# Adding expert results in DRAM instead of in SBUF: a hybrid SSD and mixture-of-experts layer on one core

## The chip, the cores and the metric

The kernel runs on one core of one Trainium2 chip. The metric is device time in microseconds (us) of one execution, here the median of three runs. The core has TensorE (PE; PEld is its weight load), VectorE (DVE), ScalarE (ACT), GpSimd (POOL) and SyncE (SP), and 16 DMA engines that all queues share. In the views a "q" behind an engine's name (SPq, POOLq) is its instruction queue: issuing a transfer or waiting.

## The reference

One inference layer over 528 prompt rows (16 learned meta rows and 512) and 64 sample rows, 592 rows of 1024 in all. The change touches only the mixture of experts at its end:

```python
def _hier_moe(h, ...):
    p_grp = softmax(t @ w_rg + b_rg);  g_sel = argmax(p_grp)          # one of 4 groups
    le = (t @ w_re + b_re)[group g_sel];  top_v, top_i = top_k(softmax(le), 2)
    top_v = top_v / sum(top_v);  gate = top_v * g_prob                # two experts of that one group
    for g in range(N_EGROUPS):
        act = silu(t @ w_gate[g]) * (t @ w_up[g]) * gate[:, g, :, None]
        out = out + einsum('tef,efd->td', act, w_down[g])
x = x + mixer ; x = x + HierMoE(RMSNorm(x)) ; final RMSNorm
```

There are 32 experts (4 groups of 8) of width 256. Every row goes to two experts, both of the same group. All data are fp32.

## The kernel before

**Stages.** Up to about 1000 us the kernel computes the projections, the short convolution and the state-space branch. Then come the output projection (added into `x2`, the residual rows in SBUF, five tiles of 128 rows, the last of 80), the router, 16 pairs of experts, and the end: summing up, the final norm, the stores.

**Router.** DVE finds the two experts of every row (`m1`, `m2`) and its place within each expert. PE multiplies the one-hot places `at_slot` with `tok_of` (L874), which gives for each slot of an expert the row that sits in it. The first 64 slots of an expert are its *main* part (`MAIN`), the next 32 its *over* part (`OVER`). From this come the indices `gid_main`, `gid_over` for gathering rows and `sid_main`, `sid_over` for scattering results. Slots without a row have an index out of bounds and move nothing, apart from one harmless row (`DUMP`). `tok_of` has two halves, since a row's first result goes to row t of `y_tok` and its second to row 640 + t. A last branch, for an expert with over 96 rows, isn't taken with these data.

**Expert pairs** (`for p in range(PAIRS)`, experts 2p and 2p + 1). PE: gate and up matmuls of main (L944), transposes of the next pair's rows (L920), gate and up of over (L957), transposes of h (L965, L973), down of main into the bank `acc[1]` (L983), down of over into `pS` (L991). ACT applies Silu and copies the transposed rows; DVE multiplies, and copies both results from PSUM to `ye_main` (L1392) and `ye_over` (L1394), double buffered. POOL gathers the rows of pair p + 3 (L1890), then scatters the main results (L1907), waits until they have landed, scatters the over results (L1911), and waits for those before it scatters for the next pair. DVE may write `ye_main` of pair p only when both scatters of pair p - 2 have landed (`ye_out`). SP loads the weights two pairs ahead: gate and up (L518) once PE has done the gate and up matmuls of pair p - 2, down (L521) once it has done its down matmuls.

**End.** When both scatters of the last pair have landed, DVE passes the branch and releases SP by `f_skip`. SP loads ten tiles (two for each tile of rows) from `y_tok` (L555). DVE computes x2 = x2 + y * gate twice for each tile (L1429), ACT the root of the mean square (L1454, L1455), DVE the normed row (L1421, L1422), and SP stores it.

**y_tok fill.** ACT fills `y_tok` once with finite numbers in four transfers during the state-space stage (L1572), DRAM to DRAM.

Of the kernel before, what the change touches and what calls it, by code (L numbers as in the profile page):

```python
# [12 lines left out]
P = 128  # L13
# [38 lines left out]
Y_ROWS, DUMP, NO_TOKEN = 640, 1232, 2048  # L52
# [7 lines left out]
def build(nc, ins, outs):  # L60
    ctx = ExitStack()
    with ctx:
# [141 lines left out]
        tokback, b = carve(b, [2, TILES], big, B5)  # L204
# [3 lines left out]
        at_slot, _ = carve(3 * WE, [2 * TILES, CAP])  # L208
        tok_of, _ = carve(24 * T, [2 * TILES, 2, NE], big, B5)
# [23 lines left out]
        y_in = [carve(D * n, [D])[0] for n in range(2 * TILES)]  # L233
# [4 lines left out]
        def expert_slot(u):  # L238
# [7 lines left out]
        y_tok = nc.dram_tensor("y_tok", [DUMP + 1, D], F32).ap()  # L246
        y_half = y_tok.rearrange("r (h c) -> (r h) c", h=2)
# [51 lines left out]
        y_fill, m_end = sem("y_fill"), sem("m_end")  # L299
# [4 lines left out]
        f_w, f_id, f_cast, f_x, f_tr, f_xe, f_gu, f_silu, f_act, f_dn, f_ye, f_out, f_skip = (  # L304
            sem(n) for n in ("f_w", "f_id", "f_cast", "f_x", "f_tr", "f_xe", "f_gu", "f_silu", "f_act", "f_dn", "f_ye",
                             "f_out", "f_skip"))
        g_in = [sem(f"g_in{i}") for i in range(TILES)]
        z_ss, z_sd, z_y, y_out = (sem(n) for n in ("z_ss", "z_sd", "z_y", "y_out"))
# [103 lines left out]
        def _(sp):  # L412
# [103 lines left out]
            def load_gate_up(e):  # L516
                for part, w in zip(wexp[e % 4][0:2], (wg, wu)):
                    sp.dma_start(part, w[e]).then_inc(gu_in[e // 2 % 2], 16)  # L518

            def load_down(e):  # L520
                sp.dma_start(wexp[e % 4][2], wd[e]).then_inc(dn_in[e // 2 % 2], 16)  # L521
# [69 lines left out]
        def _(pe):  # L591
# [275 lines left out]

            pe.wait_ge(r_sel, 1)
            for bank_, size, at, count in ((pS, MAIN, 0, 2), (pT, OVER, MAIN, 4)):
                for n in range(2):  # L870
                    for i in range(TILES):
                        r = ROWS[i]
                        for q in range(count):
                            m = nc.tensor.matmul(bank_[size * q:size * q + size, 0:2 * PAIRS], at_slot[0:r, n * TILES + i, at:at + size],  # L874
                                                 tok_of[0:r, n * TILES + i, :, q % 2:NE:2], start=n + i == 0,
                                                 stop=i == TILES - 1 and n == 1)
# [55 lines left out]
            pe.wait_ge(s_tl, 8)  # L932
            turn_main(0)
            pe.wait_ge(r_ids, 3)
            turn_over(0)
            for p in range(PAIRS):
# [39 lines left out]

                pe.wait_ge(dn_in[p % 2], 32 * (p // 2 + 1))
                if p >= 1:
                    pe.wait_ge(m_ye, 2 * (p - 1) + 1)
                for h in range(2):  # L980
                    for ft in range(FK):
                        for j in range(2):
                            m = nc.tensor.matmul(acc[1][main_of(j), h, :], hT_main[:, ft, main_of(j)],  # L983
                                                 wexp[(2 * p + j) % 4][2][:, ft, h * 512:(h + 1) * 512],
                                                 start=ft == 0, stop=ft == FK - 1)
                m.then_inc(m_dn, 1)
                pe.wait_ge(m_hc, 2 * p + 2)
                for ft in range(FK):
                    for q in range(4):
                        j, h = q % 2, q // 2  # L990
                        m = nc.tensor.matmul(pS[over_of(q), :], hT_over[:, ft, over_of(j)],  # L991
                                             wexp[(2 * p + j) % 4][2][:, ft, h * 512:(h + 1) * 512],
                                             start=ft == 0, stop=ft == FK - 1)
                m.then_inc(m_dn, 1)
# [4 lines left out]
            with pe.If(n_most > CAP):  # L999
                with pe.Fori(0, NE) as e:  # L1000
                    with pe.Fori(0, ROUNDS) as r:
                        n = e * ROUNDS + r
                        pe.wait_ge(f_x, n * 16 + 16)
                        to_rows(0, f_tr)
                        pe.wait_ge(f_w, n * 48 + 48)
                        pe.wait_ge(f_xe, n + 1)
                        gate_up(0, 0, pT, f_gu)
                        pe.wait_ge(f_act, n + 1)
                        down(0, 0, down_banks[0], f_dn)
# [3 lines left out]
        def _(dve):  # L1013
# [313 lines left out]
            for n, m_ in enumerate((m1_, m2_)):  # L1327
                link(v.tensor_tensor(tok_of[:, n * TILES:(n + 1) * TILES, 0, :], m_.rearrange(fl), wide(tokback[:, 0, :], NE), ALU.mult))
                link(v.tensor_tensor(tok_of[:, n * TILES:(n + 1) * TILES, 1, :], m_.rearrange(fl), wide(tokback[:, n, :], NE), ALU.mult))
# [16 lines left out]
            v.tensor_scalar(sid_main[:, :], pS[:, PAIRS:2 * PAIRS], float(NO_TOKEN), empty, ALU.add, ALU.min)  # L1346
            x = v.tensor_scalar(sid_f, pT[:, PAIRS:2 * PAIRS], 2.0, half, ALU.mult, ALU.add)
# [11 lines left out]
            link(v.tensor_tensor(gate[:, 1, :], gate[:, 0, :], ev, ALU.mult))  # L1359

            dve.wait_ge(r_ids, 3)
            for n, m_ in enumerate((m1_, m2_)):
# [12 lines left out]
                link(v.tensor_tensor(t_, gate[:, n, :], gate_later[:, n, :], ALU.subtract))  # L1375
                link(v.tensor_copy(gate[:, n, :], gate_later[:, n, :]))
                link(v.tensor_copy(gate_later[:, n, :], t_))
            v.tensor_copy(most[0:1, 0:1], cmax[0:1, 0:1]).then_inc(r_slot, 1)

            for p in range(PAIRS):  # L1380
# [15 lines left out]
            for s in range(2):  # L1396
                dve.wait_ge(ye_out[s], 32 * PAIRS // 2)
            n_most = dve.value_load(most[0:1, 0:1], min_val=0, max_val=T)
            with dve.If(n_most > CAP):
                with dve.Fori(0, NE) as e:  # L1400
                    with dve.Fori(0, ROUNDS) as r:
                        n = e * ROUNDS + r
                        dve.wait_ge(f_silu, n + 1)
                        v.tensor_tensor(gs[0], gs[0], pT[:, FK * CAP:2 * FK * CAP].rearrange("p (a b) -> p a b", a=FK),
                                        ALU.mult).then_inc(f_act, 1)
                        dve.wait_ge(f_dn, n + 1)
# [18 lines left out]
            for i in range(TILES):  # L1425
                r = ROWS[i]
                dve.wait_ge(g_in[i], 32)
                for n in range(2):
                    x = v.scalar_tensor_tensor(x2[0:r, i, :], y_in[2 * i + n][0:r, :], gate[0:r, n, i:i + 1], x2[0:r, i, :],  # L1429
                                               ALU.mult, ALU.add)  # L1430
                    if n == 0:
                        link(x)
                x.then_inc(z_ss, 1)
                if i >= 1:
                    finish(i - 1)
            finish(TILES - 1)
# [527 lines left out]
```

## Time and profile before

| | |
|---|---|
| median of 3 runs (lowest, highest) | 1428.02 us (1427.01, 1428.05) |
| the profiled execution: its time, its span | 1430.2 us, 1428.5 us |
| PE busy | 1324.7 us, 93% of the span |
| DVE, ACT, POOL busy | 567.5, 377.9, 457.0 us |
| DMA | 209.75 MB, mean 147 GB/s |
| mean granted clock of TensorE | 0.953 of full speed |

The span runs from the first to the last instruction. Full speed of TensorE is 2.4 GHz; a granted clock of 0.5 is its level of 1.2 GHz.

### The profile page before, as it was taken

To read this page: it belongs to the slowest core of one execution; us is meant where nothing else is said; L and a number is where in the kernel's file an instruction comes from. 1 tells how busy PE (TensorE), PEld (TensorE's weight loads), DVE (VectorE), ACT (ScalarE), POOL (GpSimd) and SP (SyncE) were. 2 spreads that over 40 slices of the span, in tenths; PEclk is the share of its full clock that TensorE was granted. 3 is DMA by queue.
4 is the path that set the end of the run, shared out by engine and by line. 5 is a ranking of instruction groups with operands and counts; after the bars stand their busy time and mean duration, and the time that the engine had idled before them with its cause. 6 is when DMAs were issued, how large, how long until landed. Compare 5 with 4: busy or idle time off the path is not lost.

```text
span 1428.5 us, 23149 instructions
## 1 busy us (share of the span) xinstructions
PE 1324.7 (93%) x9087; PEld 1027.3 (72%) x9087; DVE 567.5 (40%) x816; ACT 377.9 (26%) x574; POOL 457.0 (32%) x380
## 2 busy tenths in 40 slices
PE   4999999999989999998999999999987999999990
PEld 4999999999759877975987799994474444444430
DVE  5444441026566754955676550011153111111115
ACT  4212124344234324333342531210121111101102
POOL 5444432345333533533252454330002112122110
PEclk8999999999989999999999999999956999999995
DMA  5223222235107303520631222337612999999925
GB/s 144 75 75 87 74 68 65 78 84 151 48 13 186 109 0 110 132 65 7 182 104 43 81 74 75 89 104 267 279 49 67 363 368 374 370 360 376 378 97 203
DMA packets 179334, 209.75 MB, mean 147 GB/s; under 512 B 12988, under 2 KB 154428, under 8 KB 170896
## 3 DMA queue, kind: packets, MB, share of 16 engines
q1 hardware_dynamic: 167970, 187.97, 40.2%
q10 hardware_dynamic: 4134, 11.11, 2.2%
q0 software_dynamic: 7168, 9.81, 1.9%
q8 instruction: 44, 0.72, 0.2%
q14 instruction: 18, 0.14, 0.0%
HBM read 196.93 MB, written 32.34 MB: 160 GB/s over the span
## 4 chain that ended last, share of the span: by engine, by line
PE 75%; DVE 12%; issue 4%; ACT 3%; DMA 3%; SPq 1%; DVEq 1%; ACTq 0%; POOLq 0%; POOL 0%
PE acc L584 36%; PE pT L944 8%; PE acc L819 5%; PE pS L957 4%; PE acc L983 4%; DVE area L1149 4%; PE pY L747 2%; PE pS L991 2%; PE pS L691 2%; DMA ring<-in_w_in 1%; PE acc L920 1%; PE acc L713 1%; DVE big L1220 1%; PE pY L927 1%; PE pS L753 1%
## 5 line engine op out<-in xcount | busy, mean ns | idle before, releaser
L584 PE MATMUL acc<-h_parts,ring_parts 128*128 128x328 f32 (+1 forms) x3840 | 551.5, 305 | 12.6 <-DVE h_parts L1047 6.9
L584 PEld LDWEIGHTS acc<-h_parts,ring_parts 128*128 128x128 f32 x3840 | 537.7, 192 | 29.0 <-issue 28.2
L1736 POOL TENSOR_TENSOR ring_parts<-ring,ring_parts 128x1024 fp32r<-128x1024 f32 x104 | 263.2, 2531 | 419.3 <-ACT ring_parts L1468 419.3
L1468 ACT ACTIVATE ring_parts<-ring 128x1024 fp32r<-128x1024 f32 x104 | 110.0, 1058 | 371.1 <-PE acc L584 353.6
L944 PE MATMUL pT<-area,big 128*64 128x512 f32 x384 | 116.1, 611 | 0.2 <-ACT big L1665 0.2
L584 PE MATMUL acc<-u_parts,ring_parts 128*128 128x264 f32 (+1 forms) x640 | 109.4, 299 | 0.0
L584 PEld LDWEIGHTS acc<-u_parts,ring_parts 128*128 128x128 f32 x640 | 96.4, 188 | 0.0
L1149 DVE SCALAR_TENSOR_TENSOR area<-area,xvec 128x616 f32<-128x616 f32 x72 | 90.1, 1252 | 10.5 <-DVE area L1147 0.6
L944 PEld LDWEIGHTS pT<-area,big 128*64 128x64 f32 x384 | 35.5, 140 | 78.8 <-issue 78.8
L584 PE MATMUL acc<-area_parts,ring_parts 128*128 128x264 f32 (+1 forms) x512 | 91.1, 299 | 0.0
L584 PEld LDWEIGHTS acc<-area_parts,ring_parts 128*128 128x128 f32 x512 | 78.4, 188 | 0.0
L1890 POOL DMA_INDIRECT big<-h_rows,gid_main x16 | 16.7, 1043 | 161.9 <-DVE big L1351 107.6
L957 PE MATMUL pS<-area,big 128*32 128x256 f32 x768 | 58.5, 381 | 0.0
L983 PE MATMUL acc<-area,big 128*64 128x512 f32 x192 | 58.4, 598 | 0.0
L944 PE MATMUL pT<-ring,big 128*64 128x512 f32 x128 | 56.6, 595 | 0.0
L1677 ACT ACTIVATE big<-pT 128x256 f32<-128x256 f32 x16 | 6.1, 384 | 190.3 <-PE pT L944 190.3
L1817 POOL TENSOR_TENSOR area<-m_le,da 128x512 f32<-128x512 f32 (+1 forms) x40 | 41.1, 1031 | 47.1 <-PE pS L691 47.1
L1911 POOL DMA_INDIRECT y_tok<-big,sid_over x16 | 16.0, 998 | 125.1 <-DMA y_tok<-big,sid_main 125.1
L1240 DVE TENSOR_TENSOR area<-acc,area 128x528 f32<-128x528 f32 x8 | 5.7, 707 | 115.7 <-PE acc L584 115.7
L1382 DVE TENSOR_TENSOR big<-big,pT 128x256 f32<-128x256 f32 x16 | 6.7, 421 | 111.5 <-ACT big L1677 111.5
L691 PE MATMUL pS<-area,m_gt 128*128 128x512 f32 (+1 forms) x80 | 39.1, 570 | 12.8 <-ACT area L1581 12.8
L1180 DVE TENSOR_TENSOR area<-area 128x512 f32<-128x512 f32 (+1 forms) x40 | 35.8, 903 | 32.3 <-ACT area L1581 30.8
(332 smaller groups left out, 1708.5 us busy)
## 6 DMA issues: line engine op xcount, KB each, us to landing
ring<-in_w_in SPq DMA_DIRECT2D x80, 512.0 KB, 4.1
area<-in_w_gate SPq DMA_DIRECT2D x24, 1024.0 KB, 6.3
area<-in_w_up SPq DMA_DIRECT2D x24, 1024.0 KB, 9.3
area<-in_w_down SPq DMA_DIRECT2D x24, 1024.0 KB, 11.5
area<-in_state_ssm SPq DMA_DIRECT2D x16, 512.0 KB, 7.0
out<-area SPq DMA_DIRECT2D x16, 512.0 KB, 5.3
ring<-in_w_ssd_out SPq DMA_DIRECT2D x16, 512.0 KB, 4.2
ring<-in_w_gate SPq DMA_DIRECT2D x8, 1024.0 KB, 11.5
```

The costliest lines, as they stand in the source:

```text
L584: m = nc.tensor.matmul(acc[a][:, h, 0:n], w[s][:, k, :], x[:, k, h * HALF:h * HALF + n], start=first and k == 0 and w is w_hi and x is hi, ...
L691: nc.tensor.matmul(pS[0:r, 0:4 * r], gt[0:r, 0:r], rbuf[0:r, q, 0:4 * r], start=True, stop=True).then_inc(p_seg, 1)
L747: m = nc.tensor.matmul(pY[0:r, h * HD:(h + 1) * HD], wts[0:r, h // 4, (h % 4) * r:(h % 4 + 1) * r], xdt[0:r, i % 2, h * HD:(h + 1) * HD], ...
L819: m = nc.tensor.matmul(acc[n % 4 // 2][0:ROWS[i], n % 2, :], mT[:, k, tok(i)], wo[h][:, k, :], start=k == 0, stop=k == 7)
L944: m = nc.tensor.matmul(pT[main_of(j), :], xT_[:, k, main_of(j)], gate_up_w(2 * p + j, k), start=k == 0, stop=k == 7)
L957: m = nc.tensor.matmul(pS[over_of(q), 0:FE], xT_[:, k, at:at + OVER], wexp[(2 * p + j) % 4][n][:, k, :], start=k == 0, stop=k == 7)
L983: m = nc.tensor.matmul(acc[1][main_of(j), h, :], hT_main[:, ft, main_of(j)], wexp[(2 * p + j) % 4][2][:, ft, h * 512:(h + 1) * 512], start ...
L1149: x = v.scalar_tensor_tensor(o_, raw[:, c % 2, n:n + XCONV], w[:, 0, n:n + 1], o_, ALU.mult, ALU.add)
L1180: v.tensor_tensor(w, w, cbm[0:r, 0:r].unsqueeze(1).broadcast_to([r, 4, r]), ALU.mult).then_inc(s_w, 1)
L1468: a_.activation(w_hi[b % 2], w_raw[b % 2], ACT.Copy).then_inc(hi_done, 1)
L1736: gp.tensor_tensor(w_lo[b % 2], w_raw[b % 2], w_hi[b % 2].bitcast(F32), ALU.subtract).then_inc(lo_done, 1)
L1817: gp.tensor_tensor(rbuf[0:r, q, 0:4 * r].rearrange("p (h c) -> p h c", h=4), le[0:r, 0:r].unsqueeze(1).broadcast_to([r, 4, r]), da[0:r, i, ...
```

## The change

- Results are weighted as they leave PSUM: instead of a copy, DVE multiplies by a gate for each slot (`gate_main`, `gate_over`). Those gates come from a second selection on PE, `at_slot` times `gate_of` (m1 and m2 times the gates), 60 small matmuls into `acc[1]`, which PE runs before it transposes the first pair's rows.
- `y_tok` becomes `y_sum` with 593 rows. SP fills it with the residual rows `x2` (5 stores, and one for the spare row) after the output projection. The ACT fills go.
- Both scatters of a pair add to what stands in DRAM (`compute_op=ALU.add`).
- A pair is made of one expert of one group and one of another (`expert_of`), so that no row occurs twice in one transfer. `tok_of` has one half instead of two.
- In the last pair the over results go first and the main results second.
- At the end SP waits for the last scatters itself and loads five tiles from `y_sum` straight into `x2`. The ten weighted sums on DVE go.
- Semaphores of the branch that isn't taken are merged.

```diff
+            def expert_of(n):
+                return n // 16 * 16 + n % 2 * EPG + n // 2 % EPG
...
+            for i in range(TILES):
+                sp.wait_ge(r_x2, TILES + i + 1)
+                sp.dma_start(y_sum[tok(i), :], x2[0:ROWS[i], i, :]).then_inc(y_fill, 16)
+            sp.dma_start(y_sum[DUMP:DUMP + 1, :], x2[0:1, 0, :]).then_inc(y_fill, 16)
             for p in range(2, PAIRS):
                 sp.wait_ge(m_gu, 2 * (p - 2) + 2)
...
+            for s in range(2):
+                sp.wait_ge(ye_out[s], 32 * PAIRS // 2)
+            for i in range(TILES):
+                sp.dma_start(x2[0:ROWS[i], i, :], y_sum[tok(i), :]).then_inc(g_in[i], 16)
             sp.wait_ge(m_end, 1)
...
-            sp.wait_ge(f_skip, 1)
-            for s in range(2):
-                sp.wait_ge(ye_out[s], 32 * PAIRS // 2)
-            for i in range(TILES):
-                for n in range(2):
-                    at = n * Y_ROWS + i * P
-                    sp.dma_start(y_in[2 * i + n][0:ROWS[i], :], y_tok[at:at + ROWS[i], :]).then_inc(g_in[i], 16)
...
             pe.wait_ge(s_tl, 8)
+            pe.wait_ge(r_gate, 1)
+            for h, size, at, count in ((0, MAIN, 0, 2), (1, OVER, MAIN, 4)):
+                for n in range(2):
+                    for i in range(TILES):
+                        r = ROWS[i]
+                        for q in range(count):
+                            m = nc.tensor.matmul(acc[1][size * q:size * q + size, h, 0:PAIRS],
+                                                 at_slot[0:r, n * TILES + i, at:at + size],
+                                                 of_pairs(gate_of[0:r, n * TILES + i, :], q % 2), start=n + i == 0,
+                                                 stop=i == TILES - 1 and n == 1)
+            m.then_inc(r_gs, 1)
             turn_main(0)
...
                 pe.wait_ge(dn_in[p % 2], 32 * (p // 2 + 1))
+                if p == 0:
+                    pe.wait_ge(r_gs, 2)
                 if p >= 1:
                     pe.wait_ge(m_ye, 2 * (p - 1) + 1)
+                if p < PAIRS - 1:
+                    down_main()
+                    down_over()
+                else:
+                    down_over()
+                    down_main()
...
+            for n, m_ in enumerate((m1_, m2_)):
+                x = v.tensor_tensor(gate_of[:, n * TILES:(n + 1) * TILES, :], m_.rearrange(fl), wide(gate[:, n, :], NE), ALU.mult)
+            x.then_inc(r_gate, 1)
...
-                dve.wait_ge(m_dn, 2 * p + 1)
-                v.tensor_copy(ye_main[p % 2], acc[1].rearrange("p a b -> p (a b)")).then_inc(m_ye, 1)
-                dve.wait_ge(m_dn, 2 * p + 2)
-                v.tensor_copy(ye_over[p % 2], pS[:, :]).then_inc(m_ye, 1)
+                results = [(ye_main[p % 2], acc[1].rearrange("p a b -> p (a b)"), gate_main), (ye_over[p % 2], pS[:, :], gate_over)]
+                for n, (to, of, by) in enumerate(results if p < PAIRS - 1 else results[::-1]):
+                    dve.wait_ge(m_dn, 2 * p + n + 1)
+                    v.tensor_scalar(to, of, by[:, p:p + 1], None, ALU.mult).then_inc(m_ye, 1)
...
-                act.dma_start(y_tok[bass.ds(g * (DUMP // GROUPS), DUMP // GROUPS), :], ins["x_prompt"][0][0:DUMP // GROUPS, :]
-                              ).then_inc(y_fill, 16)
...
-                pool.indirect_dma_start(y_tok[:, :], bass.IndirectOffsetOnAxis(ap=sid_main[:, p:p + 1], axis=0),
-                                        ye_main[p % 2], None, bounds_check=DUMP, oob_is_err=False).then_inc(ye_out[p % 2], 16)
...
+                results = [(y_sum, sid_main, ye_main[p % 2], DUMP), (y_half, sid_over, ye_over[p % 2], 2 * DUMP + 1)]
+                for n, (to, index, of, bound) in enumerate(results if p < PAIRS - 1 else results[::-1]):
+                    pool.wait_ge(m_ye, 2 * p + n + 1)
+                    if n == 1:
+                        pool.wait_ge(ye_out[p % 2], 32 * (p // 2) + 16)
+                    pool.indirect_dma_start(to[:, :], bass.IndirectOffsetOnAxis(ap=index[:, p:p + 1], axis=0), of, None,
+                                            bounds_check=bound, oob_is_err=False, compute_op=ALU.add).then_inc(ye_out[p % 2], 16)
```

## Rows read from the trace of the kernel before

**Rows 1.** Chain of waits, expert stage: start us, us, what.

```profile
1127.94 7.02 PE pT L944 x32
...
1144.90 1.85 PE pS L991 x16
1146.76 7.02 PE pT L944 x32
```

**Rows 2.** By stretch: us; busy PE, PEld, DVE, ACT, POOL; clock, DMA share, GB/s.

```profile
1125.00:1200.00 75.00, 75.00 (x594) 31.92 (x592) 13.90 (x24) 9.53 (x16) 15.76 (x17) 1.00 0.93 363
...
1392.00:1394.00 2.00, 0.00 (x0) 0.00 (x0) 0.00 (x0) 0.00 (x0) 0.00 (x0) 0.86 0.36 139
```

**Rows 3.** Timeline of POOL: start us, us, what, idle before and releaser.

```profile
1109.43 1.02 POOL L1907 DMA_INDIRECT y_tok<-big,sid_main  x1 [2.92 <-DVE big L1392]
1118.64 1.00 POOL L1911 DMA_INDIRECT y_tok<-big,sid_over  x1 [8.20 <-DMA y_tok<-big,sid_main]
```

**Rows 4.** DMA, 1125 to 1300 us: a queue's share; transfers, KB, us to landing.

```profile
q0 software_dynamic: 4176, 5.78, 8.9%
...
ring<-in_w_up SPq DMA_DIRECT2D x4, 1024.0 KB, 14.3
...
y_tok<-big,sid_main POOLq DMA_INDIRECT x10, 8.5
y_tok<-big,sid_over POOLq DMA_INDIRECT x9, 3.9
```

**Rows 5.** Timeline of SP: the first load of pair 2.

```profile
1102.08 0.33 SPq L518 DMA_DIRECT2D area<-in_w_gate  x1
```

**Rows 6.** Chain of waits after the last pair's main down matmuls.

```profile
1388.44 1.24 DVE big L1392
...
1390.52 3.15 DMA y_tok<-big,sid_main
...
1394.52 3.01 DMA y_tok<-big,sid_over
...
1399.21 5.30 DMA area<-y_tok
...
1408.34 1.28 ACT L1455
...
1423.51 1.28 DVE big L1422
```

**Rows 7.** Groups of instructions: busy us, mean ns, idle before.

```profile
L1429 DVE SCALAR_TENSOR_TENSOR big<-area,gate,big 128x1024 f32<-128x1024 f32 (+1 forms) x10 | 12.8, 1282 | 13.8 <-DMA area<-y_tok 13.6
...
L1382 DVE TENSOR_TENSOR big<-big,pT 128x256 f32<-128x256 f32 x16 | 6.7, 421 | 111.5 <-ACT big L1677 111.5
```

**Rows 8.** The ten loads of L555.

```profile
DMA to landing us min/median/max: 3.9/8.0/11.9
```

**Rows 9.** Timeline of DVE: the reciprocal of one tile at the end.

```profile
1421.69 0.15 DVE L1421 RECIPROCAL stat<-stat 128x1 f32<-128x1 f32 x1
```

**Rows 10.** Chain of waits, router and first pair.

```profile
1074.51 2.35 PE pS L874 x40
1076.85 1.23 PE pT L874 x80
...
1084.32 1.96 PE acc L920 x8
...
1087.53 9.81 PE pT L944 x32
```

**Rows 11.** Timeline of DVE in the router: the second gate.

```profile
1080.25 0.16 DVE L1359 TENSOR_TENSOR gate<-gate,big 128x5 f32<-128x5 f32 x1
```

**Rows 12.** By stretch, columns as in rows 2: within the first pair's gate matmuls.

```profile
1093.00:1094.00 1.00, 1.00 (x6) 0.31 (x4) 0.00 (x0) 0.00 (x0) 0.00 (x0) 0.97 0.00 0
```

**Rows 13.** Timeline of ACT beside one fill of y_tok.

```profile
354.34 0.67 ACTq L1572 DMA_DIRECT2D y_tok<-in_x_prompt  x1
...
356.31 0.27 ACT L1577 ACTIVATE area<-pO 128x128 f32<-128x128 f32 x1
```

More of the change, by code:

```diff
@@ L514, in load_expert, with load_gate_up, load_down @@
                     sp.dma_start(part, src).then_inc(done_sem, 16)
[L516 to L521, printed above, removed]
+            def expert_of(n):
+                return n // 16 * 16 + n % 2 * EPG + n // 2 % EPG
+            def load_gate_up(n):
+                for part, w in zip(wexp[n % 4][0:2], (wg, wu)):
+                    sp.dma_start(part, w[expert_of(n)]).then_inc(gu_in[n // 2 % 2], 16)
+            def load_down(n):
+                sp.dma_start(wexp[n % 4][2], wd[expert_of(n)]).then_inc(dn_in[n // 2 % 2], 16)
             for e in (0, 3):
@@ L873, in _ @@
                         for q in range(count):
-                            m = nc.tensor.matmul(bank_[size * q:size * q + size, 0:2 * PAIRS], at_slot[0:r, n * TILES + i, at:at + size],
-                                                 tok_of[0:r, n * TILES + i, :, q % 2:NE:2], start=n + i == 0,
+                            m = nc.tensor.matmul(bank_[size * q:size * q + size, 0:PAIRS], at_slot[0:r, n * TILES + i, at:at + size],
+                                                 of_pairs(tok_of[0:r, n * TILES + i, :], q % 2), start=n + i == 0,
                                                  stop=i == TILES - 1 and n == 1)
@@ L975, in _, with down_main @@
                 m.then_inc(m_ht, 1)
+                def down_main():
+                    for h in range(2):
+                        for ft in range(FK):
+                            for j in range(2):
+                                m = nc.tensor.matmul(acc[1][main_of(j), h, :], hT_main[:, ft, main_of(j)],
+                                                     wexp[(2 * p + j) % 4][2][:, ft, h * 512:(h + 1) * 512],
+                                                     start=ft == 0, stop=ft == FK - 1)
+                    m.then_inc(m_dn, 1)
@@ new lines, in down_over @@
+                def down_over():
+                    pe.wait_ge(m_hc, 2 * p + 2)
+                    for ft in range(FK):
+                        for q in range(4):
+                            j, h = q % 2, q // 2
+                            m = nc.tensor.matmul(pS[over_of(q), :], hT_over[:, ft, over_of(j)],
+                                                 wexp[(2 * p + j) % 4][2][:, ft, h * 512:(h + 1) * 512],
+                                                 start=ft == 0, stop=ft == FK - 1)
+                    m.then_inc(m_dn, 1)
@@ L986, in _ @@
[L986 to L994, printed above, removed]
+                if p < PAIRS - 1:
[4 more added lines that the diff above has]
+                    down_main()
@@ L1345, in _ @@
                             ).then_inc(r_ids, 1)
-            v.tensor_scalar(sid_main[:, :], pS[:, PAIRS:2 * PAIRS], float(NO_TOKEN), empty, ALU.add, ALU.min)
-            x = v.tensor_scalar(sid_f, pT[:, PAIRS:2 * PAIRS], 2.0, half, ALU.mult, ALU.add)
+            v.tensor_scalar(sid_main[:, :], pS[:, 0:PAIRS], float(NO_TOKEN), empty, ALU.add, ALU.min)
+            x = v.tensor_scalar(sid_f, pT[:, 0:PAIRS], 2.0, half, ALU.mult, ALU.add)
             link(x)
@@ L1425, in _ @@
             for i in range(TILES):
[L1426 to L1436, printed above, removed]
+                finish(i)
         @block.scalar
@@ L1697, in _ @@
                         act.wait_ge(f_out, n * 16 + 17)
+            act.wait_ge(f_skip, 1)
             for i in range(TILES):
-                act.wait_ge(z_ss, i + 1)
+                act.wait_ge(g_in[i], 16)
                 root(i, x2[0:ROWS[i], i, :], sqj, z_sd)
```

81 lines of the change are left out of this document (37 added, 44 removed).

## The prediction

> **What bounds the kernel now.** Four views, in this order. The busy time by stretch first: between 1125 and 1200 us PE is busy in all 75 us at a granted clock of 1.00, and the DMA engines at a share of 0.93 [rows 2]. Two resources are nearly full, so the question is which sets the pace. The chain of waits answers: pair after pair it names matmuls alone, and the main gate matmuls of one pair start 18.8 us after those of the last (1127.94, 1146.76) [rows 1]. So PE sets the pace of the expert stage. DMA has 7% to spare there, and anything that adds DMA work or latency has to be priced against that. Third, the timeline of POOL, for the scatters: a serial chain beside PE's. Last, the chain of waits after the last matmuls, where nothing overlaps: from 1388.4 to 1428.5 us each step lies on the path [rows 6], so a microsecond there is a microsecond of the result.
>
> **The end.** Before: the main product leaves PSUM at 1388.44, its scatter starts on POOL at 1390.52 and lands 3.15 later, the over scatter starts at 1394.52 and lands 3.01 later, at 1397.5; the branch, f_skip and the issue take until 1399.21; the first tile's two loads 5.30; then two sums of 1.28 each [rows 6, 7], the square, ACT's table load of 1.28 (at 1408.34), the root, and the norms. DVE is then the limit: five tiles by two sums and a norm. The last norm starts at 1423.51, ends at 1424.8, and the last store ends the span 3.7 later.
>
> After, on the same axis. *Over first:* the over down matmuls need a copy on DVE that now hides behind the main ones. PE waits for it; a DVE pass of twice the columns takes 0.42 [rows 7], so the cost is 0 to 0.42, and I take 0.4. PE's end moves from 1388.4 + 1.85 (over, [rows 1]) = 1390.25 to 1390.65. *Main product:* 1.24 [rows 6], to 1391.9. A multiply costs DVE what a copy does: 0.42 for 256 columns read from PSUM against 1.24 for 1024 is about 1.05 ns for each further column [rows 6, 7]. *Scatter:* from the end of the copy (1389.68) to POOL's start (1390.52) are 0.84, so the start is at 1392.75. The over scatter, its data ready 3.6 earlier, lands by 1391.6 and is out of the way. *Landing:* 3.15, and what adding costs. No row shows an adding transfer. Nearest: in the 2 us about it the engines were busy for 0.36 x 2 = 0.72 us [rows 2], the rest is latency. Adding needs the destination row read before it is written. Bounds: 0, and another 3.15 (everything twice). I take 1.3, the transfer's own work once more and a little latency, since the larger part of 3.15 is not data. Landed at 1397.2. *Loads:* SP waits for nothing else and issues at 1397.3; the branch now lies beside the scatter. The quickest of the ten loads landed in 3.9 [rows 8]: first tile at 1401.2. *Norms:* square 1.2 (1407.1 to 1408.34), table load 1.28, root and reciprocal about 0.5: the first norm starts at 1404.2. Five norms, with a reciprocal of 0.15 between them [rows 6, 9], are 5 x 1.28 + 4 x 0.15 = 7.0: 1411.2. The five tiles are half the bytes of the ten, whose last landed 11.9 after its issue; even that (1409.2) would delay the end by about 1. Store 3.7: **1414.9, that is 13.6 earlier**.
>
> **Router.** The first selection (L874) lies on the path with 2.35 + 1.23 = 3.6 [rows 10], and its moving columns go from 32 to 16. Halved it gives 1.8, unchanged 0. The second selection has as many matmuls of the same shape, so costs PE 1.8 to 3.6. It can start when the gates (1080.41) and two DVE products of about 0.32 are done, at 1081.1 [rows 11], and PE is idle until 1084.32, when the first rows have come [rows 10]. At 3.6 it ends at 1084.7, 0.4 too late; with both halved all moves up by 1.8. I take -0.3, near the unchanged end, because the per-matmul cost there (59 ns of main against 15 of over, at the same columns) follows the number of tiles side by side and not the columns. The two gate copies and the shorter slot bookkeeping on DVE end before DVE is next wanted (about 1097).
> The first pair's gate matmuls take 9.81 instead of 7.02, because the clock was granted in full only from about 1093 [rows 1, 10, 12]. PE, idle before 1084.32, now works there, so the rise may come sooner: 0 to 2.8 gained, I take 0.
>
> **Taken at nothing.** *ACT fills:* 0.67 each in ACT's queue, four of them, so at most 2.7. The issue ends at 355.0 while the next ACT work starts only at 356.31, behind earlier work of ACT without a gap [rows 13]; I take 0. *The five stores and one row into y_sum:* they move to SP after the early weights and before the loads of pair 2, which SP issues at 1102.08 [rows 5]; x2 is final at about 1036.5. Cover is 65 us; behind them in SP's queue is only that load. *Multiply instead of copy:* above. *Weights:* the gate and up weights of a pair are issued from 1102.08, land within 14.3 of issue, and are needed at 1127.94 [rows 1, 4, 5]: about 10 us of slack. The scatters are about half of the 8.9% of the software queue [rows 4]; moved once more they add 4.5 points to 93, at three times the work 9, to 102: 2% of 280 us is 6 us of drift, still under the slack. So bandwidth alone costs nothing.
>
> **The serial chain of scatters** is the disputed step. Main starts at 1109.43, 0.87 after its product; over starts at 1118.64, when main has landed, and lands in 3.9 [rows 3, 4]. So a pair's chain is 0.87 + 9.21 + 3.9 = 14.0 of 18.8 us: 4.8 to spare. Of main's 9.2, 4.0 are there without load too (1390.52 to 1394.52, [rows 6]), and 5.2 are waiting among the weights' packets. Bounds for adding: 0, and everything twice (28). I take 1.3 and 0.5 more, C = 15.8: hidden. The Trainium skill (DMA: Bandwidth & Descriptors, section Queues, rings and completion order) says that each engine takes turns between queues by whole packets; by that the 5.2 should stay if an added row stays one packet. No row here shows it. Against the change it says (Collectives: The Full Stack, Part 3, on the bandwidth ceiling) that a reducing transfer runs at half the rate of a copy, since it reads two sources. By that an all-data transfer would double, and the sum here would be 0.6 us less at the end (0.72 instead of 1.3), or, if the contended time doubles with it, the first rival below.
>
> **Sum.** 1428.5 - 13.6 - 0.3 = 1414.6 for the span. The profiled execution took 1430.2, and the median of the runs, 1428.02, is 0.5 below its span, so **1414**.
>
> **Rivals.**
> 1. *The chain of adding scatters becomes the bound: slower.* POOL issues a pair's scatter only after the last one landed. 14 chains lie beside weight loads, two behind them without (about 9.3 each). The last landing is at 1108.6 + 14C + 18.6, which equals the planned 1397.2 at C = 19.3; each us above costs 14, and at C = 20.3 the gain is gone. For it: DMA at 0.93, and 5.2 of main's 9.2 being contention. If that doubles (+5.2, and 0.9 for over) on top of my 1.8, C = 21.9: 1127.2 + 306.6 = 1433.8, 37 later: about 1450. Against: the scatters are small, and a late PE loads weights later, which frees DMA.
> 2. *Adding costs its latency at the end:* 3.15 for main instead of 1.3, and an over scatter landing 3.0 later, which holds main by 2.7: 4.6 more, 1419. For it: nothing there is hidden. Against: only 0.72 of the 3.15 are data.
> 3. *The end gives more:* the clock rises early (2.8), both selections halve (1.5 more), adding free (1.3): down to 1408.4.
> 4. *No change:* the tail's gain would have to be eaten by a chain with C just at 20.3.
>
> **Chances.** Forecast (1409 to 1418) 0.63; rival 2 and a chain slightly late (to 1425) 0.14; rival 3 0.04; rival 1 0.16; rival 4 0.03. The range 1408 to 1425 holds 0.81. A change under 0.2% (2.9 us) is about what a measurement of this kernel can't tell from none. Faster 0.80, within 0.03, slower 0.17.
>
> **What would show it.** In the profile after: pair period still 18.8 with PE busy throughout; POOL's wait between main and over scatter near 9 and not above 14; no wait of DVE for ye_out; between the last main product and the first load to `x2` about 5.4 us; no gap on DVE from the first norm to the last but for reciprocals; the first transpose of rows near 1084. Wrong if PE waits in the expert stage, or if the last landing is later than 1399.

## The result, and the profile after

The changed kernel took 1417.88 us (median of 4 runs, 1416.39 to 1419.62), beside 1428.03 for the kernel before on the same chip: a ratio of 0.9934 [0.9922, 0.9946]. Forecast were 1414 (1408 to 1425) and faster. The medians differ by 10.2 us where 14.0 was forecast. Its profiled execution took 1419.62, its span 1417.8, so the span is 10.7 shorter than before. Medians in this document are of fast runs; the slow executions beside the experiments are left out (1515.55 and 7296.75 us of the changed kernel, 2211.74 and 2211.97 of the kernel before).

Where these 10.7 us come from is read at four points of the two chains of waits. First the router and the first pair of the kernel after (start us, us, what), the answer to [rows 10]:

```profile
1075.04 2.32 PE pS L883 x40
1077.37 1.20 PE pT L883 x80
...
1081.64 2.84 PE acc L948 x56
1084.48 0.45 issue
1084.93 0.31 PE acc L948 x5
1085.24 0.41 issue
1085.66 1.05 PE acc L948 x58
1086.71 1.92 PE acc L929 x8
...
1089.88 9.03 PE pT L964 x32
```

L883 is the first selection (before: L874), L948 the new second one, L929 the first transposes, L964 the first pair's gate matmuls. The first selection is as long as before (3.5 us). The second fills 5.1 us, with two gaps in it for which the trace shows no cause, and the transposes start when it ends: 1086.71 instead of 1084.32. The clock gives some back (9.03 for the gate matmuls instead of 9.81). All told, from the start of the selection to the end of those matmuls it is 23.9 us instead of 22.8: 1.0 lost. (Below, "the stretch" is this time.)

The pairs then follow each other as before; the last gate matmuls start at 1374.24 (before 1372.46). That is 1.8 late: 0.5 was there when the selection started, 1.0 is the router's, 0.2 a single stall of PE.

Then the end, in the same chain, the answer to [rows 6]:

```profile
1374.24 7.02 PE pT L964 x32
...
1388.93 3.61 PE acc L1001 x16
...
1392.56 1.30 DVE big L1430
...
1394.60 5.93 DMA y_sum<-big,sid_main
...
1400.61 3.59 DMA big<-y_sum
...
1405.45 1.28 ACT L1483
...
1407.27 1.28 DVE big L1460
...
1412.84 1.28 DVE big L1460
```

From the last gate matmuls to the end of the span it is 43.56 us, where before it was 56.04: 12.5 gained. With the 1.8 lost ahead of it that is the result, 10.7. One adding scatter stands where two plain ones did, and it takes 5.93 instead of 3.15; one quick load follows, and DVE does five norms and no sums.

The scatters beside the weight loads, from the timeline of POOL after (columns as in [rows 3]; L1935 issues both):

```profile
1111.00 1.63 POOL L1935 DMA_INDIRECT y_sum<-big,sid_main  x1 [2.92 <-DVE big L1430]
...
1168.93 1.60 POOL L1935 DMA_INDIRECT y_sum<-big,sid_main  x1 [4.17 <-DVE big L1430]
1179.38 1.57 POOL L1935 DMA_INDIRECT y_sum<-big,sid_over  x1 [8.86 <-DMA y_sum<-big,sid_main]
...
1189.77 1.60 POOL L1935 DMA_INDIRECT y_sum<-big,sid_main  x1 [6.18 <-DMA y_sum<-big,sid_over]
...
1343.53 1.60 POOL L1935 DMA_INDIRECT y_sum<-big,sid_main  x1 [4.44 <-DMA y_sum<-big,sid_over]
...
1376.48 1.55 POOL L1935 DMA_INDIRECT y_sum<-big,sid_main  x1 [2.96 <-DMA y_sum<-big,sid_over]
1383.61 1.55 POOL L1935 DMA_INDIRECT y_sum<-big,sid_over  x1 [5.58 <-DMA y_sum<-big,sid_main]
1390.63 1.55 POOL L1935 DMA_INDIRECT y_sum<-big,sid_over  x1 [5.47 <-DVE big L1430]
```

Look at what ended the wait in brackets. At first a main scatter waits for its data (DVE). From the fifth pair on it waits for the over scatter of the pair before: the chain of scatters is now slower than PE. Twelve intervals take 1343.53 - 1111.00 = 232.5, that is 19.4 each against PE's 18.81, and the chain is 6.8 us late by then. PE never notices. When the weight loads have ended, the chain takes 14.5 (1361.97 to 1376.48) and catches up: the last over scatter waits for DVE again.

Last the DMA view, 1125 to 1300 us, and the busy time by stretch, the answers to [rows 4] and [rows 2]:

```profile
q0 software_dynamic: 4464, 5.23, 12.1%
...
y_sum<-big,sid_main POOLq DMA_INDIRECT x9, 9.6
y_sum<-big,sid_over POOLq DMA_INDIRECT x9, 8.5
```

```profile
1125.00:1200.00 75.00, 74.87 (x594) 31.81 (x592) 14.37 (x24) 9.54 (x16) 19.63 (x16) 1.00 0.97 362
```

The share went from 0.93 to 0.97, and the over scatter's landing from 3.9 to 8.5 us. POOL is busy 1.6 us for an adding scatter, 1.0 for a plain one.

### The profile page after: what moved, and what is told of

The parts are those of the page before. It is cut to its first block, busy times and chain, and to the rows that moved or that the text cites. A ratio compares the mean times of both kernels' runs of the same rounds, so it can differ in the third digit from the quotient of the medians.

```text
span 1417.8 us, 23366 instructions
## 1 busy us (share of the span) xinstructions
PE 1328.1 (94%) x9207; PEld 1029.9 (73%) x9207; DVE 555.9 (39%) x804; ACT 377.6 (27%) x574; POOL 477.4 (34%) x379
## 4 chain that ended last, share of the span: by engine, by line
PE 76%; DVE 12%; issue 4%; ACT 3%; DMA 3%; SPq 1%; DVEq 1%; ACTq 0%; POOLq 0%
PE acc L590 36%; PE pT L964 8%; PE acc L825 5%; PE pS L977 4%; PE acc L1001 4%; DVE area L1181 4%; PE pS L1011 2%; PE pY L753 2%; PE pS L697 2%; DMA ring<-in_w_in 1%; PE acc L929 1%; PE acc L719 1%; DVE big L1252 1%; PE pS L759 1%; PE pY L936 1%
## 5 line engine op out<-in xcount | busy, mean ns | idle before, releaser
L964 PE MATMUL pT<-area,big 128*64 128x512 f32 x384 | 115.3, 606 | 0.2 <-ACT big L1691 0.2
L964 PEld LDWEIGHTS pT<-area,big 128*64 128x64 f32 x384 | 35.2, 139 | 78.2 <-issue 78.2
L1935 POOL DMA_INDIRECT y_sum<-big,sid_over x16 | 25.1, 1568 | 129.0 <-DMA y_sum<-big,sid_main 115.7
L964 PE MATMUL pT<-ring,big 128*64 128x512 f32 x128 | 56.6, 595 | 0.0
L697 PE MATMUL pS<-area,m_gt 128*128 128x512 f32 (+1 forms) x80 | 39.1, 570 | 12.8 <-ACT area L1607 12.8
L1935 POOL DMA_INDIRECT y_sum<-big,sid_main x16 | 25.5, 1596 | 73.1 <-DMA y_sum<-big,sid_over 57.5
```

The lines of the kernel that those rows point to most:

```text
L697: nc.tensor.matmul(pS[0:r, 0:4 * r], gt[0:r, 0:r], rbuf[0:r, q, 0:4 * r], start=True, stop=True).then_inc(p_seg, 1)
L964: m = nc.tensor.matmul(pT[main_of(j), :], xT_[:, k, main_of(j)], gate_up_w(2 * p + j, k), start=k == 0, stop=k == 7)
L1935: pool.indirect_dma_start(to[:, :], bass.IndirectOffsetOnAxis(ap=index[:, p:p + 1], axis=0), of, None, bounds_check=bound, oob_is_err=Fals ...
```

## The experiments

Medians of the kernel before beside the experiments were 1427.70, 1428.17 and 1427.03, on three chips. Single executions of it lay between 1425.51 and 1431.17 there, so a difference of 1 or 2 us between two medians of a few runs says little, and the stretches of the profiles say more. "The end" below runs, as above, from the last pair's gate matmuls to the end of the span.

**The changed kernel once more, twice** (on the chips of the other kernels).

> The changed kernel once more, unedited. Its four runs so far lie in two clusters, 1416.4 to 1416.7 and 1419.1 to 1419.6 us. Theory A: the second selection on PE, 5.1 us in the first profile with two gaps of 0.4 us in which PE waits for nothing that the profile shows, is sometimes shorter; then a profile of the quick cluster has the first rows' transposes begin near 1084 instead of 1086.7. Rival: the end varies, by the landing of the last adding scatter (5.9 us); then the span from the last down matmuls to the end differs and the router doesn't. Either way a median of 1416 to 1419.

> The changed kernel unedited, beside the versions below on the same chip: 1413 to 1420 us. Theory: its profile shows one of two forms of the second selection, without gaps (3.6 us, the first rows' transposes 10.2 us after the first selection began, the first pair's gate matmuls at 7.1) or with two gaps of 0.4 us (transposes at 11.7, gate matmuls at 9.0), 3.4 us apart in the end. Rival: a third form in between.

1414.09 (0.9905 [0.9888, 0.9921]) and 1414.23 (0.9903 [0.9886, 0.9919]); spans 1413.4 and 1412.7. The first is 2 us below the 1416 to 1419 that was expected. The end takes 44.2 and 43.7, so it is 11.8 to 12.5 shorter than before in the three profiles. Of the 4.4 us between the spans 1417.8 and 1413.4, the selection starts 1.4 earlier, and 3.4 are the router, which is alike in both new profiles; the first one's chain of waits:

```profile
1073.60 2.32 PE pS L883 x40
...
1080.19 3.58 PE acc L948 x119
1083.78 1.90 PE acc L929 x8
...
1086.93 7.09 PE pT L964 x32
```

The second selection runs without gaps, in 3.58, and the gate matmuls take 7.09, at full clock. Here the change's router is 20.4 us from selection to the end of those matmuls: 2.4 quicker than before, where the first profile is 1.0 slower. So the same program has two forms there, 3.4 us apart. The form with gaps is in the first profile and in all four taken on the chip of the experiments with adding in one scatter, the over scatter twice and main first; the form without is in all four on the two other chips that run this selection unedited. Whether it goes by the execution or by the chip is open.

The first four runs (1419.62, 1419.06; 1416.69, 1416.39) lie in two groups too, but the forms don't explain such groups. The runs of the first repetition also lie in two (1412.87, 1413.01; 1415.16, 1415.75), and its profile, of 1415.16, is of the slower group and has no gaps. The kernel without the second selection (below) has 1413.39 to 1414.61 and then 1418.37, 1418.59. A part of such spread lies ahead of the change: the start of the first selection varies from 1070.95 to 1075.16 us between profiles.

The kernel before isn't fixed in this stretch either. Its version with the pairs alone changed (last experiment) takes 21.1 there, with its first rows 9.2 us after the selection's start instead of 9.8 and gate matmuls of 8.69 instead of 9.81. Against that profile the change's router costs 2.8 with gaps and wins 0.7 without.

**Without adding.**

```diff
-   bounds_check=bound, oob_is_err=False, compute_op=ALU.add)
+   bounds_check=bound, oob_is_err=False)
```

> Both scatters of every pair write plainly instead of adding (the sum over experts and residual is left out of the output). Theory: adding costs only at the end, where nothing hides it: POOL's issue 1.0 instead of 1.55 and the last main landing 3.2 instead of 5.9, so 2.8 us faster than the changed kernel, about 1414 to 1415; the serial chain of a pair's scatters falls from 19.3 us to 14, with no effect on PE. Rival: the chain at 19.3 us already holds PE up a little somewhere, then the gain is over 4 us.

1412.49, 0.9892 [0.9877, 0.9907]; span 1411.5, 1.9 below the unedited one on that chip (medians: 1.6), where 2.8 was expected. Mains are 18.8 apart again, and the over scatter lands in 3.6. Its end (chain of waits):

```profile
1389.62 4.55 DMA y_sum<-big,sid_main
...
1394.23 3.63 DMA big<-y_sum
```

The last main scatter lands in 4.55 here even plain, and in 5.93 to 6.59 with adding in the three unedited profiles: 1.4 to 2.0 apart. But this pair of numbers doesn't price adding by itself. The main scatter one pair earlier also has no weight loads beside it, and there main goes before over, as in the kernel before. Its landing in the DMA views, first without adding (1369.6 to 1374.6 us), then in the changed kernel (1376 to 1384 us):

```profile
y_sum<-big,sid_main POOLq DMA_INDIRECT x1, 3.2
```

```profile
y_sum<-big,sid_main POOLq DMA_INDIRECT x1, 6.3
```

There adding costs 3.1, and 2.7 to 3.1 over all profiles in which main adds (5.9 to 6.3): the landing nearly doubles. With adding the place makes no clear difference (5.93 to 6.59 in the last pair, 6.26 with main first in the last pair too); a plain scatter is slower behind the over scatter (4.55) than ahead of it (3.2). Why is open. The DMA view over the 5 us after the last main scatter's start, first the changed kernel's, then the one without adding:

```profile
q0 software_dynamic: 136, 0.31, 43.8%
```

```profile
q0 software_dynamic: 144, 0.32, 17.5%
```

The engines are busy with it for 2.2 us with adding (43.8% of 5 us, with 8 of its 144 packets still to come) and 0.9 without.

**Without the second selection.**

```diff
-            pe.wait_ge(r_gate, 1)
-            for h, size, at, count in (...):     # its matmuls
...
+            v.memset(gate_main, 0.5)
+            v.memset(gate_over, 0.5).then_inc(r_gs, 1)
...                                           # and the two copies of the gates go
```

> Without the second selection on PE; all gates are a constant (the weighting by the router is left out of the output). Theory: the selection ends 2.4 us after the first rows have landed, and its whole excess is on the path, less about 0.8 of an earlier clock that the work before buys back: 1.6 to 2.4 us faster than the changed kernel, 1415 to 1416.5. Rival: it is free, since the first rows come no earlier with their gathers, and the time is that of the changed kernel.

1414.34, 0.9919 [0.9903, 0.9935]; span 1411.5. Beside the unedited 1414.09 on that chip nothing is won in the median, where 1.6 to 2.4 was expected from the form with gaps. Chain of waits:

```profile
1071.60 2.32 PE pS L883 x40
...
1078.03 2.65 DMA big<-h_rows,gid_over
1080.68 0.14 issue
1080.82 1.96 PE acc L929 x8
...
1084.02 8.41 PE pT L953 x32
```

Now the transposes wait for the gathered rows, 9.2 after the selection's start; they come 10.2 after it in the clean form and 11.7 in the other. Against this profile the selection is therefore not hidden, it costs 1.0 or 2.5 there (against the 9.8 of the kernel before, 0.4 or 1.9). But the gate matmuls take 8.41, as PE's clock rises later (granted 0.64 at 1086 to 1087; 1.00 from 1086 in the unedited kernel's clean form). The whole stretch is 20.8, against 20.4 clean and 23.9 with gaps: the selection is worth -0.4 or +3.0.

**Half of the second selection moved behind the transposes** (the main part stays ahead, the over part of 40 matmuls goes behind `turn_over(0)`).

```diff
-            for h, size, at, count in ((0, MAIN, 0, 2), (1, OVER, MAIN, 4)):
+            for h, size, at, count in ((0, MAIN, 0, 2),):
...
             turn_over(0)
+            for h, size, at, count in ((1, OVER, MAIN, 4),):
```

> The main part of the second selection stays ahead of the first rows' transposes, the over part moves behind them, where PE waits 1.2 us for ACT's copy. Theory: the main part (2.8 us) fits under the landing of the first gather and the over part (1.1 us of work) under ACT's copy: 1.5 to 2.2 us faster than the changed kernel. Rival: the two gaps of 0.4 us come from fetching PE's instructions and move with them, then under 1 us is won.

1415.98, 0.9916 [0.9903, 0.9928]; span 1414.6; the stretch is 21.3, where the form without gaps has 20.4. The transposes come 9.05 after the selection's start, but the moved part then takes 1.26 in front of the gate matmuls, and these 7.99. Nothing of the expected 1.5 to 2.2 is won: moving it returns work to the path.

**Adding in one of the two scatters.**

```diff
-   bounds_check=bound, oob_is_err=False, compute_op=ALU.add)
+   bounds_check=bound, oob_is_err=False, **(dict(compute_op=ALU.add) if to is y_sum else {}))
```

That is for the main scatters alone; for the over scatters alone it reads `if to is y_half`.

> Only the main scatters add, the over scatters write plainly (their part of the sum is left out). In the changed kernel the over scatter takes 8.5 us to land beside the weight loads, 3.6 when both write plainly. Theory A (adding itself makes it slow): here over lands in about 4 us, and the chain of a pair is about 15.5 us. Theory B (it is issued later, behind a slower main scatter, into the next pair's loads): it still lands in about 8 us, and the chain stays near 19.

> Only the over scatters add, the main scatters write plainly (their part of the sum is left out). Theory A (adding itself makes over slow): over lands in about 8.5 us although it is issued as early as in the kernel before, and the chain is about 18. Theory B (timing): over lands in about 4 us. The last main scatter, plain and without load, lands in about 4.5 us instead of 5.9 to 6.6 in both.

One execution each: 1418.76 (span 1417.0) and 1415.43 (1413.6). Landings, 1125 to 1300 us, in the DMA views, first with only main adding, then with only over:

```profile
y_sum<-big,sid_main POOLq DMA_INDIRECT x10, 9.7
y_sum<-big,sid_over POOLq DMA_INDIRECT x9, 5.0
```

```profile
y_sum<-big,sid_main POOLq DMA_INDIRECT x10, 8.3
y_sum<-big,sid_over POOLq DMA_INDIRECT x9, 4.1
```

An over scatter that adds lands in 4.1 when it starts where it did before. So the 8.5 of the changed kernel is not the price of adding in it. Main lands in 9.3 to 9.7 under load where it adds and in 8.3 to 8.6 where it doesn't (over all profiles so far), so its price there is 0.7 to 1.4. What is left for the 8.5 is where the over scatter falls. From the timelines of POOL and SP, 1195 to 1240 us, its start against SP's first gate load beside it, and its median landing:

| kernel | over scatter starts | landing, us |
|---|---|---|
| without adding | 1.8 to 2.6 ahead of the load | 3.6 |
| before | 1.7 to 2.4 ahead | 3.9 |
| only over adds | 2.2 to 2.7 ahead | 4.1 |
| only main adds | 1.3 to 1.9 ahead | 5.0 |
| changed kernel | 1.4 to 2.9 behind | 8.5 |

The landing follows the place more than the adding. The table alone leaves a rival, since its one late scatter also adds; two views of single scatters settle it. In the changed kernel itself the first over scatter, which adds like all others, starts 1.4 ahead of its load (at 1121.06) and lands in 3.7, the third 0.65 ahead and lands in 8.5. And with only main adding, the plain over scatter slides from 1.5 ahead in the first pair to 1.9 behind in the thirteenth; at 1310.42 it starts 0.65 behind (DMA view, 1310 to 1312 us):

```profile
y_sum<-big,sid_over POOLq DMA_INDIRECT x1, 7.4
```

So a plain one is slow there too, and mains are 19.0 apart in that kernel, as Theory B has it; with only over adding they are 18.8 apart. The gathers that POOL now issues 1.9 behind the over scatter aren't needed for it: at 1353.48, in the changed kernel, none follows, and the landing is 7.7. The place isn't all, though: with only over adding, three landings from 1287 us on took 6.7 to 7.8, although the scatters started 1.4 to 2.1 ahead. Open.

Both profiles have the gaps in the router. The 3.4 us between them are 1.2 ahead of the selection, 0.8 in the pairs (PE waits three times for DVE) and 1.4 at the end, where main adds in one (43.7) and not in the other (42.3).

**The over scatter twice, in pairs 0 to 14** (the over results are then added twice).

```diff
+                    if n == 1 and p < PAIRS - 1:
+                        pool.indirect_dma_start(to[:, :], ..., compute_op=ALU.add).then_inc(x_more, 16)
+                        pool.wait_ge(x_more, 16 * (p + 1))
```

> In pairs 0 to 14 the over scatter is issued twice, each waiting for the one before (over results are counted twice in the output): the chain is longer by one adding scatter, 4 to 9 us, so 23 to 28 us of a pair's 18.8. Theory (rival 1 of the prediction: from 19.3 us on each microsecond costs 14): POOL falls behind, DVE waits for ye_out and PE with it; +50 us at the least (C of 23), +120 at the most. Rival: the lateness is absorbed by the double buffer and by transfers that get quicker when PE is late; then under 15 us are lost.

1478.83, 1.0361 [1.0340, 1.0382]; span 1474.9. The chain is 24.7 a pair (mains at 1109.2 to 1405.1, 12 intervals), and now others wait for it. By stretch, 1125 to 1300, and waits over the same time (total, times, longest):

```profile
1125.00:1300.00 175.00, 160.99 (x1210) 67.35 (x1208) 28.02 (x48) 19.05 (x32) 49.79 (x38) 0.95 0.85 318
```

```profile
DVE big L1431 <- DMA y_sum<-big,sid_over: 61.6, 5, 15.9
...
PEld acc L930 <- DMA big<-h_rows,gid_over: 18.3, 5, 5.8
```

DVE waits for a free `ye_main`, PE idles 14 of 175 us, and DMA is used less (0.85), so no bandwidth is short: it is the serial chain. 12 x (24.7 - 19.4) = 63 us, and the span is 57 to 62 longer than the three of the unedited kernel. Rival 1 is a real mechanism. How far below its edge the changed kernel sits isn't measured: no run lies between 19.4 and 24.7.

**Main first in the last pair too.**

```diff
-                if p < PAIRS - 1: ...
-                else:
-                    down_over()
-                    down_main()
+                down_main()
+                down_over()
```

> The last pair in the order of all others, main before over. Theory: PE ends 0.4 us earlier and the main results leave PSUM 1.9 us earlier, but the over scatter (about 3 us with its issue) is then behind the main one and not hidden: the last landing comes 1.1 us later after the last matmul began, 1 us slower in all. Rival: it makes no difference, or wins, since the adding main scatter is the long one and gets the earlier start.

1420.53, 0.9943 [0.9924, 0.9961]; span 1419.3. Chain of waits:

```profile
1392.16 6.26 DMA y_sum<-big,sid_main
...
1399.23 2.89 DMA y_sum<-big,sid_over
```

The end is 45.2, which is 1.0 to 1.7 more than in the three unedited profiles, where 1.1 was expected. Over first is worth that much of the 12.5.

**The root's table loaded early**, and the same with the half selection moved.

```diff
             act.wait_ge(f_skip, 1)
+            a_.activation(stat[0:1, 3, 0:1], eps[0:1, :], ACT.Sqrt)
```

> ACT computes one square root of a single number before it waits for the first tile, so that its table load of 1.28 us lies beside the last scatter and not behind the first tile's square. Theory: ACT and through it the first norm come 1.28 us earlier and DVE stays the limit behind it: 1.3 us faster than the changed kernel. Rival: the tiles' landings become the limit (each 512 KB takes about 1.3 us, as long as a norm), and under 0.7 us is won.

> Both edits: over part of the second selection behind the first transposes, and the early square root. In the profile of the split alone the transposes came 1.1 us earlier than in the quick form of the changed kernel, but the first pair's gate matmuls took 8.0 instead of 7.1 us since the clock rose later. Theory: the split wins nothing against the quick form and 2.5 us against the form with gaps, so about the time of the early root alone, or up to 2.5 us less where that has gaps. Rival: the split is faster in every form, by the 1.1 us.

1414.01 (0.9899 [0.9883, 0.9916]) and 1414.83 (0.9909 [0.9893, 0.9926]), beside 1414.23 for the unedited kernel. The 1.28 us of the table load do leave the path; timeline of ACT with the early load:

```profile
1391.22 1.28 ACT L1725 ACT_TABLE_LOAD   x1 [9.63 <-PEq L1029]
...
1400.86 1.06 ACT L1482 ACTIVATE big<-big 128x1024 f32<-128x1024 f32 x1 [8.14 <-DMA big<-y_sum]
...
1405.41 1.06 ACT L1482 ACTIVATE big<-big 128x1024 f32<-128x1024 f32 x1 [0.34 <-DMA big<-y_sum]
```

but ACT then comes to the fourth tile before its load has landed, which took 6.9 us. The loads are next in line: 0.34 us of wait here, 0.91 in the other kernel. The end is 43.0 and 43.5 in these two, beside 43.7 unedited on that chip: 0.7 and 0.2 of 1.28 arrive in the profiles, and nothing in the medians.

**Only the pairing, in the kernel before.**

```diff
-                    sp.dma_start(part, w[e]).then_inc(gu_in[e // 2 % 2], 16)
+                    sp.dma_start(part, w[expert_of(e)]).then_inc(gu_in[e // 2 % 2], 16)
...                                           # the down loads and the first selection's columns alike
```

> The kernel before with the pairing of experts of different groups alone. Theory: no difference, within 0.1%: the same 16 pairs of loads and matmuls in another order. Rival: the loads come from places in DRAM that suit the DMA better or worse, then the weights' landing times differ from before's 6 to 14 us; PE would not see it.

1426.92, 0.9998 [0.9988, 1.0008]. The order of the experts costs nothing. The end is 56.0 again and the last main scatter lands in 3.20, so neither the 12.5 nor the 4.55 above comes from the new pairs. Pairs from one group with adding scatters weren't tried, since a row can then occur twice in one transfer.

## Why the prediction was right, and where its terms were off

**The end: right in place, 1.1 too much.** Forecast 13.6 gained, measured 12.5 (11.8 and 12.3 in the other two profiles). Term by term, forecast then measured: PE's end after the last gate matmuls 18.2, 18.3; main product 1.25, 1.32; to POOL's start 0.85, 0.74; landing 4.45, 5.93; to the load 0.1, 0.07; load 3.9, 3.59; root 3.0, 3.07; five norms 7.0, 6.85; store 3.7, 3.7. Only the landing was mis-sized, and the load was 0.3 better. No run takes out the ten loads and the ten sums alone; that the gain is theirs is read from the two chains, in which every other term keeps its size.

The step that failed here is "I take 1.3, the transfer's own work once more and a little latency, since the larger part of 3.15 is not data". Adding nearly doubled the whole landing, not its data alone, where main goes before over as in the row of 3.15 (3.2 without adding, 5.9 to 6.3 with it). So 1.3 was 1.5 too small for the first profile's 5.93, and the upper bound, "everything twice" (6.3), was nearly met. Rival 2 had this landing right. It cost less than rival 2's 1419, since its second half, over holding main, did not occur: the over scatter started at 1390.63, 4.0 ahead of main, and main did not wait for it.

The Trainium skill (Collectives: The Full Stack, The bandwidth ceiling: the fold count and why AG ≠ RS ≠ AR) has a reduce-scatter between cores at half the rate of an all-gather, since the add reads two sources. Taken over to this scatter, an estimate from the 0.9 us of engine time would be 1.8; this case shows at least 2.2, so the measurement decides.

**Router: the step that failed.** What I took was that the second selection would hide in PE's idle time. "PE is idle until 1084.32" holds for that profile, and so does "costs PE 1.8 to 3.6" for the form without gaps (3.58). That form starts the transposes 10.2 after the selection's start, 0.4 later than the kernel before: it is the case of my own sum, "At 3.6 it ends at 1084.7, 0.4 too late", and not the -0.3 that I took. With the gaps it is 1.9 later. The first selection did not halve (3.5 us for 3.6), as taken. "The rise may come sooner: 0 to 2.8 gained, I take 0" was open and was 2.7 in one form (9.81 to 7.09), 0.8 in the other. Net -2.4 or +1.0 where I had -0.3. The sign of this term isn't settled, since the kernel before varies in the stretch too (22.8 and 21.1). What makes the gaps stays open: they come after 56 or 57 recorded matmuls in the profiles that have them.

**The chain of scatters: right outcome, wrong number.** "I take 1.3 and 0.5 more, C = 15.8: hidden" failed. Measured is 19.4: 14.0 before, 1.1 more for main's landing (9.6 for 8.5) and 4.6 more for over's (8.5 for 3.9) give 19.7, near enough. Main's 1.3 was nearly right. I priced over by adding alone, and adding is 0.5 of it, as forecast (4.1 for 3.6 in the runs). What I missed is that main's extra time pushes over's start from ahead of the next loads to behind them, and that the chain, once late, stays there. Rival 1 needed the contended part of main's landing to double; it didn't (without loads 6.3, with them 9.6).

My own threshold (19.3) was reached, and the rival's price did not fall due for two reasons that the trace shows. Only some 12 intervals are under load, and behind them the chain takes 14.5 a pair, which wins the 7 us back: POOL waited 5.47 for DVE before the last over scatter. That the chain stayed hidden was luck as far as my reasoning goes, which had it 3.6 us a pair shorter. Issuing over twice added 5.3 a pair and cost 57 to 62 us: 11 to 12 for each us of C, where the rival had 14.

**Taken at nothing, and nothing:** bandwidth (0.93 to 0.97, PE busy 74.87 of 75); the multiply (1.30 for 1.24); the pairing, in the run above. The fills and the stores gave no visible gain or loss, but the start of the last stretch before the router varies by 5.6 us between kernels with the same code ahead of it (964.0 to 969.6), so less than that can't be told.

**The sum.** Forecast 1414.6 for the span; measured 1417.8 in the first profile (upstream 0.5, router 1.3, stall 0.2 and end 1.1 over forecast) and 1413.4 and 1412.7 in the other two. The medians of the three, 1417.88, 1414.09 and 1414.23, all lie above 1414, but against the kernel before on the same chip the gain is 10.2, 13.6 and 12.8 for a forecast of 14.0. That the last two come so near is partly chance: an end 1.3 to 1.8 worse than forecast and a router 2.1 better. Of the signs I named, one misled: the last landing at 1400.54 is "later than 1399", though by 1.5 us only, and without a wait of PE behind it.

## What to carry to other kernels

Work that moves from DVE into an adding transfer pays where nothing overlaps, at the end, and costs there about 3 us of landing (5.9 to 6.6 for 3.15). Price the whole landing of an adding transfer again, not only its data (3.2 became 5.9 to 6.3 here). In a stage that is full, ask not only what the transfer itself costs but which loads its new start collides with, and how much of a serial chain's slack that eats. Before any such move, compute the chain's period against the bound's period and count for how many rounds it runs under load: being late by 0.6 us a round was harmless for 12 rounds here, and in 50 it would come to 30 us, more than a pair's 18.8 (an estimate, no run here has it). A stretch of PE idle time is cover for work only until its end, and a short burst in it may cost its own length or give back as much through the clock, so give such a term both signs. Take more than one profile of each kernel before a term of 1 to 3 us is believed.

## What the runs showed of the hardware that was not expected

- An adding indirect scatter keeps POOL busy 1.6 us for 1.0, holds the DMA engines at least 2.2 us for 0.9, and with no loads beside it lands in 5.9 to 6.3 for 3.2.
- A plain main scatter that lands in 3.15 to 3.2 ahead of the over scatter lands in 4.55 behind it, with no weight loads beside it. With adding the two places don't differ. Open.
- The over scatter takes 3.6 to 4.1 us to land when it starts 2 us ahead of the next weight loads, and 8.5 when it starts 2 us behind them. Behind them it takes 6.8 to 7.4 without adding too.
- One program's burst of 60 small matmuls (119 records) runs in 3.58 us or in 5.07 with two gaps of 0.4 us. Without gaps the granted clock is full from 1086 us on, with them it was 0.50 until 1093 in the first profile. By stretch there:

```profile
1090.00:1093.00 3.00, 3.00 (x8) 0.96 (x10) 0.00 (x0) 1.60 (x2) 1.94 (x2) 0.50 0.21 52
```
